# Stick-breaking blocks: the causal mask as GpSimd selections in the sigmoids' results, or as a product that adds it to the scores

## What is computed

```python
def stick_breaking_attention(q, k, v):          # 8 heads, 1024 rows, blocks of 128 queries
    def block(args):                            # qi: 128 queries, i: number of the block
        qi, i = args
        t_pos = i * Q_BLOCK + jnp.arange(Q_BLOCK)
        z = jnp.einsum('bhqd,bhkd->bhqk', qi, k) * scale
        causal = s_pos[None, :] < t_pos[:, None]               # strictly causal
        log_1m = jnp.where(causal, jax.nn.log_sigmoid(-z), 0.0)
        after = lax.cumsum(log_1m, axis=3, reverse=True) - log_1m
        w = jnp.where(causal, jnp.exp(jax.nn.log_sigmoid(z) + after), 0.0)
        return jnp.einsum('bhqk,bhkd->bhqd', w, v)
```

## Time and profile before

| | us |
|---|---|
| median of 3 runs (lowest 1059.06, highest 1063.85) | 1059.1 |
| the profiled execution | 1059.08 |
| its span, from the first to the last instruction | 1057.2 |

### The profile page before, as it was taken

How to read it: one execution, slowest core, us unless ns; L and a number is a source line. 1 busy time by engine, 2 the same in 40 slices (tenths; PEclk the granted TensorE clock), 3 DMA queues, 4 the chain that set the end, 5 groups by cost and what they waited for, 6 DMA issues and landing times.

```text
span 1057.2 us, 16215 instructions
## 1 busy us (share of the span) xinstructions
PE 1020.9 (97%) x5816; PEld 913.5 (86%) x5816; DVE 680.6 (64%) x1272; ACT 632.4 (60%) x1232; POOL 96.6 (9%) x74
## 2 busy tenths in 40 slices
PE   6999999999999999999999999999999998799998
PEld 5989989899899998998998998998988986687887
DVE  4655675765856756667557549789789686667210
ACT  5658775766767757758667667567567555344000
POOL 1210201101111011011011000011011010000000
PEclk9999999999999999999999999999999998899999
DMA  8245152331432413314314204214224137822941
GB/s 247 77 115 143 29 144 54 99 102 46 128 85 60 133 48 95 105 51 127 93 31 126 75 20 120 61 29 118 55 48 130 31 100 199 253 61 76 308 130 40
DMA packets 112944, 105.50 MB, mean 100 GB/s; under 512 B 10048, under 2 KB 83784, under 8 KB 112864
## 3 DMA queue, kind: packets, MB, share of 16 engines
q1 hardware_dynamic: 110432, 104.42, 35.7%
q10 hardware_dynamic: 2432, 0.05, 0.1%
HBM read 62.44 MB, written 19.98 MB: 78 GB/s over the span
## 4 chain that ended last, share of the span: by engine, by line
PE 75%; DVE 11%; DMA 6%; ACT 4%; issue 3%; SPq 1%; ACTq 0%; DVEq 0%
PE psP L1215 37%; PE psO L1307 8%; PE psT L1289 6%; PE psS L1267 4%; PE psS L1268 4%; PE psP L1219 3%; PE psP L1325 3%; PE psP L1355 2%; PE psS L1355 2%; DVE big L999 2%; PE psT L1237 2%; DVE pt L1130 2%; PE psO L1355 2%; DMA stack<-stack 1%; DVE rb L1119 1%
## 5 line engine op out<-in xcount | busy, mean ns | idle before, releaser
L1215 PE MATMUL psP<-big 128*128 128x384 f32 (+1 forms) x2304 | 479.6, 346 | 2.2 <-DVE big L999 1.5
L1215 PEld LDWEIGHTS psP<-big 128*128 128x128 f32 x2304 | 395.9, 189 | 9.2 <-DVE big L999 1.8
L1130 DVE TENSOR_TENSOR pt<-psT,pt 128x512 fp32r<-128x512 f32 (+1 forms) x224 | 143.3, 642 | 143.9 <-ACT pt L941 143.0
L941 ACT ACTIVATE pt<-psT 128x512 fp32r<-128x512 f32 (+1 forms) x224 | 125.0, 558 | 121.7 <-PE psT L1289 120.8
L1219 PE MATMUL psP<-big 128*128 128x512 f32 x576 | 157.4, 405 | 0.0
L1307 PE MATMUL psO<-pt,vst 128*128 128x512 f32 (+3 forms) x576 | 140.7, 344 | 9.7 <-DVE pt L1130 9.2
L1289 PE MATMUL psT<-identr,z 128*128 128x128 f32 x816 | 125.9, 273 | 0.0
L1307 PEld LDWEIGHTS psO<-pt,vst 128*128 128x128 f32 x576 | 99.4, 189 | 22.2 <-issue 10.9
L1219 PEld LDWEIGHTS psP<-big 128*128 128x128 f32 x576 | 102.0, 189 | 17.7
L1289 PEld LDWEIGHTS psT<-identr,z 128*128 128x128 f32 x816 | 101.9, 140 | 15.6 <-issue 0.2
L1103 DVE CUSTOM_DVE_ANT_0 z<-psS,rb 128x640 f32<-128x640 f32 (+7 forms) x128 | 89.4, 699 | 37.4 <-PE psS L1268 18.8
(11 more groups left out here) (113 smaller groups left out, 1095.8 us busy)
## 6 DMA issues: line engine op xcount, KB each, us to landing
stack<-stack SPq DMA_DIRECT2D x192, 128.0 KB, 2.3
wraw<-in_w_in_dram SPq DMA_DIRECT2D x90, 192.0 KB, 2.7
wraw<-in_w_in_dram SPq DMA_DIRECT2D x24, 256.0 KB, 3.7
mixed_scratch<-mst SPq DMA_DIRECT2D x24, 256.0 KB, 2.7
mixed_scratch<-gate SPq DMA_DIRECT2D x24, 256.0 KB, 3.1
wraw<-in_w_out_dram SPq DMA_DIRECT2D x24, 256.0 KB, 3.5
rb<-decay_scratch SPq DMA_DIRECT2D x8, 512.0 KB, 4.0
big<-mixed_scratch SPq DMA_DIRECT2D x8, 512.0 KB, 7.0
```

The lines of the kernel that those rows point to most:

```text
L941: nc.scalar.activation(pt[:, ci % PTR, 0, 0:w], psT[:, m % NT, 0:w], ACT.Copy).then_inc(s_hi, 1)
L1130: nc.vector.tensor_tensor(pt[:, ci % PTR, 1, 0:w], psT[:, m % NT, 0:w], pt[:, ci % PTR, 0, 0:w].bitcast(F32), ALU.subtract).then_inc(s_eva ...
L1215: ins = nc.tensor.matmul(dst[:, 0:TOKW - first], hT[a][:, k, i * P:(i + 1) * P], wpair[b][:, k, first:TOKW], start=(k == 0 and q == 0), st ...
```

## The change

In the stick-breaking group TensorE no longer adds the mask to the scores. GpSimd writes it into the results of the two sigmoids instead: 1.0 into rb where the key is not before the query, in the last 128 columns of the block, and 0.0 into z. A selection in rb waits for the first sigmoid (which now has a semaphore of its own, s_sigr), the one in z for the second. VectorE's scan waits for the selection in rb (s_cutr) instead of the second sigmoid, and the multiplication for the selection in z (s_cut). The selections of a block stand at its "scores" step in GpSimd's order, and each step of GpSimd waits for the end of the one before. The forgetting group keeps its product. `item_cost` counts nothing for the mask in the stick-breaking group now, which moves some steps of PLAN past each other.

```diff
     if kind == "scores":
         n = step[1]
         total = sum(2 * max(109, w * 0.449) for _, _, w in score_parts(n)[1])
-        return total + (0 if group(n) == 1 else 59)
+        return total + (59 if group(n) == 2 else 0)
...
-POOL_KIND = [s for s in PLAN if s[0] in ("square", "sq", "gatew") or (s[0] == "norm" and s[1] >= NORMED)]
+POOL_KIND = [s for s in PLAN if s[0] in ("square", "sq", "gatew") or (s[0] == "norm" and s[1] >= NORMED)
+             or (s[0] == "scores" and s[1] >= NSOFT)]
...
+                if kind == "scores" and step[1] >= NSOFT:
+
+                    n = step[1]
+                    at, w = z_at(n)
+                    pool.wait_ge(s_sigr, n - NSOFT + 1)
+                    own = rb[:, n % 2, SEQ - P:SEQ]
+                    nc.gpsimd.affine_select(out=own, in_=own, compare_op=ALU.is_gt, fill=1.0, base=0, pattern=[[-1, P]],
+                                            channel_multiplier=1).then_inc(s_cutr, 1)
+                    pool.wait_ge(s_sig, n - NSOFT + 1)
+                    own = z[:, at + w - P:at + w]
+                    nc.gpsimd.affine_select(out=own, in_=own, compare_op=ALU.is_gt, fill=0.0, base=0, pattern=[[-1, P]],
+                                            channel_multiplier=1).then_inc(s_cut, 1)
...
-                    nc.scalar.activation(rb[:, n % 2, SEQ - w:SEQ], src, ACT.Sigmoid)
+                    nc.scalar.activation(rb[:, n % 2, SEQ - w:SEQ], src, ACT.Sigmoid).then_inc(s_sigr, 1)
...
-                    dve.wait_ge(s_sig, i + 1)
+                    dve.wait_ge(s_cutr, i + 1)
...
                     dve.wait_ge(s_rem, i + 1)
+                    dve.wait_ge(s_cut, i + 1)
...
-                        masked = group(n) != 1 and last
+                        masked = group(n) == 2 and last
```

More of the change, by code:

```diff
@@ L339 @@
     _t += turns_of(_s)
-POOL_KIND = [s for s in PLAN if s[0] in ("square", "sq", "gatew") or (s[0] == "norm" and s[1] >= NORMED)]
+POOL_KIND = [s for s in PLAN if s[0] in ("square", "sq", "gatew") or (s[0] == "norm" and s[1] >= NORMED)
+             or (s[0] == "scores" and s[1] >= NSOFT)]
 POOL_BEHIND = {}
-_n = {"square": 0, "sq": 0, "norm": 0, "gatew": 0}
+_n = {"square": 0, "sq": 0, "norm": 0, "gatew": 0, "scores": 0}
 for _i, _s in enumerate(POOL_KIND):
@@ L511, in build @@
         s_pn = sem("s_pn")
+        s_sigr = sem("s_sigr")
         s_sig = sem("s_sig")
+        s_cutr = sem("s_cutr")
+        s_cut = sem("s_cut")
         s_rem = sem("s_rem")
@@ L727, in _ @@
             nc.gpsimd.memset(rb[:, :, SEQ:SEQ + 1], 1.0).then_inc(s_const, 1)
-            done = {"const": s_const, "square": s_rs, "sq": s_rn, "norm": s_qc, "gatew": s_gmul}
+            done = {"const": s_const, "square": s_rs, "sq": s_rn, "norm": s_qc, "gatew": s_gmul, "scores": s_cut}
             for step in PLAN:
@@ L1270, in _ @@
                             end = off + P * (b + 1)
-                            m0 = 1 - (group(n) == 2)
-                            ins = nc.tensor.matmul(psS[:, end - P:end], identb[:, :], mask[:, m0:m0 + P],
+                            ins = nc.tensor.matmul(psS[:, end - P:end], identb[:, :], mask[:, 0:P],
                                                    start=False, stop=True)
```

## The result

The changed kernel takes 1063.3 us against 1059.8 for the kernel before in the same rounds (medians of 22 runs each). The ratio is 1.0026 with a 95% interval of 1.0017 to 1.0035, so about 2.8 us slower. The forecast was 1061.5, which is 2.4 slower. The interval does not reach 1: the kernel is slower, by less than the 0.5% that the prediction asks for before it calls a kernel slower. The profiled execution took 1062.66 us, with a span of 1060.9 (before 1059.08 and 1057.2).

A forecast was written before the change was run, and what follows sets the result against it. TensorE was taken to set the pace in the stick-breaking blocks. From 1059.1 us: -2.9 masks, +5.1 gate multiplications, 0 selections, +0.2 end gave 1061.5, range 1055.5 to 1067 (likeliest case 1059 to 1064).

The forecast's parts named there:

- The masks' places: TensorE, stick-breaking blocks: 64 mask products gone save 0.045 us each, 2.9 us; bounds 2.6 to 5.0.
- The gate's multiplications: GpSimd, pairs 8 to 10: two multiplications late behind selections cost 1.7 us a pair, 5.1 in all (3.3 to 6.9).
- That leaves 0 to 0.6 more: Second gate multiplication: after VectorE's 1.31 us idle and TensorE's own lateness, 0 to 0.6 us more delay; taken as 0.3.
- The selections on VectorE: VectorE sharing ports with GpSimd: 128 selections hold it by 0; bounds 0 and 0.29 us each.
- the 0.38: Product behind a VectorE scan: held 0.38 us less than GpSimd's 1.04 multiplication, so a waiting 0.29 selection fits in.
- Rival 3: Every selection stops VectorE for 0.29 us by exclusive port use: 9.2 us more, 1070.7; chance 0.07.
- The copies: GpSimd's q and k copies at a pair's start, now behind block 1's selections: 0; 0.3 us a pair with one more wait.
- The end: Program end, TensorE waiting for the last DMA of mixed results: a later last block costs 0.2 us.
- The moved steps: TensorE's order changes in pair 11 alone, by single products; no cost counted.
- Rival 1: Gate multiplications do no harm to TensorE and only the masks count: 1056.4 us; chance 0.22.
- Rival 2: Second gate multiplication comes through in full, 3.0 us in each of three pairs, 9.0 in all: 1065.4; chance 0.16.
- Rival 4: On TensorE the next weight load fills the masks' places and nothing is saved: 1064.4 us; chance 0.07.

The follow-up runs named there:

- e3_no_mask: Kernel before with no causal mask at all in the stick-breaking group, neither products nor selections: 1056.4 us, 0.9962 of the kernel before.
- e1_gate_early: Changed kernel with both multiplications of the next pair's gate weights put ahead of block 4's selections in GpSimd's order: 1056.8 us, 0.9971 of the kernel before.
- e8_first_early: Changed kernel with only the first of each pair's two gate-weight multiplications put early, the second left behind block 7's selections: 1059.6 us, 0.9988 of the kernel before.
- e5_early_old_costs: Changed kernel with both gate-weight multiplications early on GpSimd and item_cost as in the kernel before: 1055.8 us, 0.9956 of the kernel before.
- e6_early_twice: Changed kernel with both gate-weight multiplications early and every selection made twice, 256 in place of 128: 1057.0 us, 0.9966 of the kernel before.
- e2_both_early: Changed kernel with both gate-weight multiplications and the second copies of q and k ahead of the selections: 1056.3 us, 0.9969 of the kernel before.
- e10_order_only: Kernel before with only item_cost as in the changed kernel, masks still on TensorE: 1061.0 us, 1.0006 of the kernel before.
- e9_old_costs: Changed kernel with only item_cost as in the kernel before: 1061.5 us, 1.0008 of the kernel before.

## Why the prediction was right

The balance, in the run's own terms, is -4.0 for the masks, +5.8 for the late multiplications and +0.6 to +1.9 for the moved steps, in sum +2.4 to +3.7, with +2.8 measured. The prediction's 2.4 was -2.9 + 5.1 + 0 + 0.2. Its main term held. Two others were too small, in opposite directions: the masks by 1.1, the moved steps by 0.6 to 1.9. That they made up for each other was luck, and the sum is closer than its parts deserve.

- **The masks' places: 2.9 predicted, 4.0 measured** (e3_no_mask, interval 2.7 to 5.3; bounds of the prediction 2.6 to 5.0). The step that failed is "so 0.04", the reading of the mask's place as the step from it to the next product alone. The step behind that one is 0.26 instead of 0.175. Gross it is 0.11 a mask on the mean over pairs 8 to 10 and net 0.08 there, where I took 0.045. The eight masks behind narrow scores, which I put at 0.13 in the upper bound, are the cheap ones, 0.07.
- **The gate's multiplications: 5.1 predicted, 5.5 by the trace of pairs 8 to 10 and 5.8 by the runs** (e1_gate_early against the changed kernel). Its mechanism was right in each link. ScalarE idles 1.06 and 2.70 before its two L827 (predicted 1 to 1.7 and 2 to 3), TensorE's waits for the rest copies grew from 2.6 to 9.1 (predicted about 8), at the last value product of the first unit and two blocks on. Of the growth 5.7 us are theirs; the rest, up to 0.4 at a place, comes with the masks gone, in e3_no_mask too. The parts were less exact: by the timelines the first is worth 1.1 us a pair and not 1.4, the second 0.8 and not 0.3 (e8_first_early; the runs' 1.3 and 0.6 don't settle it). "That leaves 0 to 0.6 more" failed for the second: VectorE's 1.31 of idle is used up and TensorE still waits 0.82.
- **The selections on VectorE: 0 predicted, nothing measured at the end** (e1_gate_early and e3_no_mask have the same slope to block 10 of pair 8, e5_early_old_costs and e3_no_mask are equal by the runs, and e6_early_twice keeps it with twice the selections). The reasoning by the 0.38 came out where it was taken from, at the product behind a scan: the selection that waited for the scan ends at 819.32, L1139 starts at 819.27 and takes 1.09 as before. Elsewhere a selection does hold the VectorE instruction that starts during it, by up to 0.10 us, 1.1 in all, and TensorE doesn't see it. Rival 3 was wrong in its price, not in its mechanism. GpSimd is the one that waits: the selection at 823.19 takes 2.27 us and ends 0.08 after the scan that began at 823.00. GpSimd's sum for the 128 selections is 67.7 us and not the 37 predicted. A longer instruction of GpSimd holds VectorE for longer: the multiplication from 814.47 on stretches L1166 to 1.49 from the 0.69 of the earlier trace rows. The Trainium skill (SBUF — State Buffer, the section on who interferes with whom) says that the ports that the two engines share are an exclusive lock, which whoever issues first has for its whole instruction while the other is fully blocked. The traces agree in both directions, with one difference in size: VectorE goes on 0.14 before GpSimd's instruction ends, so that no selection costs it the full 0.29.
- **The copies: 0 predicted, nothing measured** (e2_both_early; in the timelines their new place is 0.4 us better over pairs 8 to 10).
- **The end: 0.2 predicted, next to nothing seen.** TensorE's wait for the last mixed results is 0.40 us after and 0.37 before; no run isolates the term.
- **The moved steps: 0 predicted, 0.6 to 1.9 us measured**, hardly clear of the runs' noise (e10_order_only, e5_early_old_costs, e9_old_costs). "The moved steps change TensorE's order in pair 11 alone, by single products" was true of TensorE (VectorE's order changes there too: the weights of block 5 now stand behind a sum with the residual) and was priced at nothing without asking what stood at each moved place. One of them is the longest wait of TensorE in the whole stretch, and what had been hidden in it came out.
- **Rivals.** Rival 1 (no harm) fails by the waits before L827. Rival 2 (the second multiplication in full) was right that there is more to it, but it is 0.8 a pair and not 3.0. Rival 4 fails by e3_no_mask and by the steps after: the next product starts about where the mask did.
- **TensorE's clock** itself did not change: the granted clock is 1.00 (2.4 GHz) in 632 to 856 us before and after, and on the mean 0.93 in 856 to 957 us in both, by two stretches of 6.8 us at 0.50. But in the changed kernel the transposes that left the long wait fall into the second of them.

## What to carry to other kernels

Before work goes to an idle engine, look at what that engine did early because it was idle: a step in the same in-order queue that ran some 10 us ahead of need becomes late once it stands behind something that waits for the present. Here the fix costs nothing: the multiplications are put ahead of the selections they don't need, and 2.8 us lost become 3.1 won. A step that is removed is priced by the start-to-start of several products behind it, not by the first alone. And where a cost in a planner changes, each step that moves past a long wait is to be looked at by itself.

## What the hardware showed that I had not expected

- A 128-wide product with weights of its own, between 384-wide ones, takes 0.04 us of the stream itself and lengthens the step behind the next product by 0.085 (0.260 against 0.174). In fp32r it is 0.059 and 0.055, so the narrower type gains nothing.
- A selection of 128x128 on GpSimd is 0.29 us alone and up to 2.27 while VectorE scans, and the 64 of them in z average 0.61.
- GpSimd's 1.04 us multiplication holds VectorE's product by 0.80, a selection of 0.29 holds a VectorE instruction by 0.12 at the most. In both cases VectorE goes on 0.14 us before GpSimd's instruction ends.
- Four transposes take 0.35 us of TensorE's stream at a granted clock of 1.00 and 0.70 at 0.50, so work that leaves a long wait can come back at twice its length.
